# Leaving the future blocks out of the causal attention and the pooling of the mix stage

## The reference, cut to what matters

```python
def pool_mixer(u, w_pool, pool_scale):     # u: (B, S, 512), four groups, windows 2, 4, 8, 16
    for gi, w in enumerate(POOL_WINDOWS):
        # mean over the last w tokens (this one included) minus the token itself
        outs.append(((cs - prev) / cnt - ch).astype(u.dtype))
    mixed = jnp.einsum('bsgc,gcd->bsgd', pooled, w_pool)
    return mixed.reshape(B, S, POOL_WIDTH) * pool_scale

def dilated_branch(q, k, v, rel_bias, window, dil):
    """Causal attention over keys at distances 0, dil, 2*dil, ..., window."""
    ...
    band = (rel >= 0) & (rel <= w_sub)     # rel = query position minus key position
    s = jnp.where(mask, s, NEG_INF)
    ...

x = x + jnp.einsum('bse,ed->bsd', jnp.concatenate([a_out, b_out], axis=-1), w_out[i])
```

## Time and profile before

| | us |
|---|---|
| median of 3 runs | 2039.34 (2037.64 to 2043.03) |
| the profiled execution, its own time | 2040.03 |
| its span, first to last instruction | 2038.3 |
| TensorE busy | 1965.7 (96% of the span) |
| VectorE busy | 747.8 |
| ScalarE busy | 425.6 |
| mix stage, input product to the last output product | about 962 to 1070.5 |
| experts | about 1084.7 to 1995.8 |

### The profile page before, as it was taken

How to read it: one execution, slowest core, us unless ns; L and a number is a source line. 1 busy time by engine, 2 the same in 40 slices (tenths; PEclk the granted TensorE clock), 3 DMA queues, 4 the chain that set the end, 5 groups by cost and what they waited for, 6 DMA issues and landing times.

```text
span 2038.3 us, 26505 instructions
## 1 busy us (share of the span) xinstructions
PE 1965.7 (96%) x10834; PEld 1056.4 (52%) x10834; DVE 747.8 (37%) x2087; ACT 425.6 (21%) x1083; POOL 100.1 (5%) x84
## 2 busy tenths in 40 slices
PE   8999999999999999999999999999999999899997
PEld 7754567885865566885463333333333333333334
DVE  4569675212768677212143222211222122112213
ACT  2161465211042465211121000000000000000003
POOL 0021220000022121000000000000000000000000
PEclk9999999999999999999999999999999999999999
DMA  7633212343543312345859999999999999999992
GB/s 252 244 138 125 84 43 84 124 165 124 207 165 124 114 53 71 116 146 194 301 203 384 427 428 428 430 429 428 429 431 428 431 428 432 431 427 427 427 421 94
DMA packets 98820, 552.29 MB, mean 271 GB/s; under 512 B 8686, under 2 KB 13202, under 8 KB 77715
## 3 DMA queue, kind: packets, MB, share of 16 engines
q1 hardware_dynamic: 98706, 550.66, 67.1%
HBM read 547.43 MB, written 3.21 MB: 270 GB/s over the span
## 4 chain that ended last, share of the span: by engine, by line
PE 81%; DMA 16%; DVE 2%; ACT 1%; issue 1%; SPq 0%; DVEq 0%; ACTq 0%
PE bank L647 28%; DMA region<-w_gate_up_dram 15%; PE bank L1232 14%; PE bank L1264 8%; PE bank L770 6%; PE bank L1006 3%; PE bank L991 3%; PE bank L1175 2%; PE bank L1161 2%; PE bank L1090 1%; PE bank L1219 1%; DMA region<-w_in_dram 1%; PE bank L850 1%; PE bank L907 1%; PE bank L874 1%
## 5 line engine op out<-in xcount | busy, mean ns | idle before, releaser
L647 PE MATMUL bank<-region 128*128 128x256 f32 (+2 forms) x2352 | 607.6, 419 | 8.2 <-DMA region<-w_in_dram 4.4
L647 PEld LDWEIGHTS bank<-region 128*128 128x128 f32 x2352 | 442.1, 191 | 162.5 <-issue 110.3
L1232 PE MATMUL bank<-region 128*64 128x512 f32 x1872 | 415.0, 597 | 24.0 <-DMA region<-w_gate_up_dram 23.2
L1232 PEld LDWEIGHTS bank<-region 128*64 128x64 f32 x1872 | 130.8, 137 | 304.0 <-issue 262.3
L2339 DVE TENSOR_SCALAR region<-bank 128x512 f32<-128x512 f32 x32 | 22.1, 691 | 681.0 <-PE bank L1232 681.0
L1264 PE MATMUL bank<-region 128*64 128x512 f32 x944 | 209.9, 595 | 9.5 <-issue 8.0
L1264 PEld LDWEIGHTS bank<-region 128*64 128x64 f32 x944 | 77.1, 137 | 122.8 <-issue 122.8
L770 PE MATMUL bank<-region 128*128 128x512 f32 x256 | 129.2, 607 | 0.0
L1674 ACT ACTIVATE region<-region 128x512 f32<-128x512 f32 x32 | 20.2, 630 | 512.4 <-DVE region L2339 512.4
L1678 ACT ACTIVATE region<-bank 128x512 f32<-128x512 f32 x32 | 19.1, 597 | 326.8 <-PE bank L1264 326.8
L1835 DVE SCALAR_TENSOR_TENSOR region<-region,layer_mem 128x256 f32<-128x256 f32 x192 | 78.0, 477 | 0.0
(11 more groups left out here) (347 smaller groups left out, 1942.8 us busy)
## 6 DMA issues: line engine op xcount, KB each, us to landing
region<-w_gate_up_dram SPq DMA_DIRECT2D x32, 4096.0 KB, 39.0
region<-w_down_dram SPq DMA_DIRECT2D x59, 2048.0 KB, 34.3
region<-w_gate_up_dram SPq DMA_DIRECT2D x53, 2048.0 KB, 21.3
region<-w_in_dram SPq DMA_DIRECT2D x44, 2048.0 KB, 8.0
layer_mem<-w_gate_up_dram SPq DMA_DIRECT2D x11, 2048.0 KB, 35.1
region<-w_out_dram SPq DMA_DIRECT2D x6, 2048.0 KB, 8.4
layer_mem<-w_down_dram SPq DMA_DIRECT2D x5, 2048.0 KB, 36.1
region<-rows_scratch SPq DMA_DIRECT2D x4, 2048.0 KB, 9.3
```

What stands on the lines that cost most here:

```text
L647: mm = pe.matmul(dst, lhs(k), w(k), start=(k == 0), stop=(k == n_k - 1))
L1232: mm = pe.matmul(pb[g][hf * 64:(hf + 1) * 64, :], XT[:, 2 * (j % 2) + kk, j // 2, :], wj[:, kk, c:c + NB], start=(first and j == 0 and kk ...
```

## The change

`pair_pT` turns three of the four 128x128 blocks of each head: (kt, t) = (0, 0), (0, 1), (1, 1). They stand side by side in the first 384 columns of the bank, and `pair_aT` copies 128x384 where it copied 128x512. `pair_out` takes one key tile for the first query tile and two for the second. `pooling` takes the product of the second token tile over output tokens 128 to 255 only. Nothing else differs.

```diff
+CAUSAL = ((0, 0), (0, 1), (1, 1))
...
                 for m in range(2):
-                    for kt in range(NT):
-                        for t in range(NT):
-                            c = (kt * 2 + t) * P
-                            mm = pe.transpose(pb[(7, 0)[m]][:, c:c + P], p2[i % 2][:, m * 512 + t * S + kt * P:m * 512 + t * S + (kt + 1) * P], ident)
+                    for kt, t in CAUSAL:
+                        c = (kt + t) * P
+                        mm = pe.transpose(pb[(7, 0)[m]][:, c:c + P], p2[i % 2][:, m * 512 + t * S + kt * P:m * 512 + t * S + (kt + 1) * P], ident)
                 mm.then_inc(s("at_pT_ps"), 1)
...
                 for t in range(NT):
                     for m in range(2):
-                        mm = product(pb[1][:, t * P + m * 64:t * P + (m + 1) * 64], lambda kt: aT2[:, m * 4 + kt * 2 + t, :],
-                                     lambda kt: z2[:, 3, kt, i * P + m * 64:i * P + (m + 1) * 64], NT)
+                        mm = product(pb[1][:, t * P + m * 64:t * P + (m + 1) * 64], lambda kt: aT2[:, m * 3 + kt + t, :],
+                                     lambda kt: z2[:, 3, kt, i * P + m * 64:i * P + (m + 1) * 64], t + 1)
                 mm.then_inc(s("at_o_ps"), 1)
...
                 for g in range(4):
-                    mm = product(pb[2 + g // 2][:, (g % 2) * S:(g % 2 + 1) * S], lambda t: z2[:, 0, t, g * P:(g + 1) * P],
-                                 lambda t: band[:, t, g, :], NT)
+                    at = (g % 2) * S
+                    for t in range(NT):
+                        mm = pe.matmul(pb[2 + g // 2][:, at + t * P:at + S], z2[:, 0, t, g * P:(g + 1) * P], band[:, t, g, t * P:S],
+                                       start=(t == 0), stop=(t == 1), skip_group_check=True)
                 mm.then_inc(once("pool_ps"), 1)
...
                 for m in range(2):
-                    last = act.activation(aT2[:, 4 * m:4 * m + 4, :], units(pb[(7, 0)[m]][:, :]), ACT.Copy)
+                    last = act.activation(aT2[:, 3 * m:3 * m + 3, :], units(pb[(7, 0)[m]][:, 0:3 * P]), ACT.Copy)
                 last.then_inc(s("at_pT"), 1)
```

## The result

The changed kernel is slower, and the prediction was wrong in sign. Its median is 2043.49 us over 12 runs (2041.80 to 2048.05), that of the kernel before, run beside it, 2039.89 over 12 (2037.64 to 2043.03): a ratio of 1.0022, 95% interval 1.0014 to 1.003. The difference of the medians is 3.60 us. Forecast were 2035.9 and at most 2040.3.

A forecast was written before the change was run, and what follows sets the result against it. The prediction took the expert weight stream, started by TensorE's progress out of the mix stage, as the bound. Terms of 0.22 + 0.84 + 1.73 + 0 + 0.44 + 0.21 = 3.44 us took 2039.34 to 2035.9 us, range 2033.0 to 2040.3.

The forecast's parts named there:

- What bounds the kernel: Expert stage: the last expert ends when the weight stream ends, and that stream's start hangs on TensorE leaving the mix stage.
- pooling: Mix stage: four matmuls, eight instructions, halved to 128 columns; gain 0.84 us, bounds 0 and 0.9.
- each output product: Mix stage, `pair_out`: each of four pairs drops two matmuls, four instructions; gain 0.43 us each, 1.73 in all.
- transposes: Mix stage, `pair_pT`: each pair drops two; gain 0.22 us for the first pair, 0.44 for third and fourth together.
- the second pair's: Mix stage, second pair's transposes: gain 0, as the wait for ScalarE's last mixed row grows from 0.35 to 0.57 us.
- the copies: Mix stage, ScalarE's copies of turned weights: only the fourth pair's two count; gain 0.21 us, 0 to 0.25.
- isolated gap for a 64-column matmul: Output product: the skill's rule gives 29 ns each, for an estimated whole sum of about 2.2 us; set aside.
- Behind the mix stage the residual, the router and the first expert keep their lengths and start 3.4 us sooner: Behind the mix stage: the 3.4 us won passes on whole, also to the tile issued at 1088.40.
- No load or queue is moved past another: Mix stage: SyncE's waits come 1.5 to 3.4 us sooner, with nothing queued behind them in the DMA until 1069.71.
- The rival with the clock: Thinned mix stage: granted clock falls, 1.69 us a spell; from three spells slower, 2041.0 us; chance 0.07.
- The range: Whole kernel: 2033.0 to 2040.3 us, from a gain of 2.4 to 3.9 us, run scatter and the absorbed case.
- What would show it wrong: Clock under 1.00 from 1020 to 1085 us, pooling waiting for VectorE, full DMA queue at 1084, or last weight wait unmoved.

The follow-up runs named there:

- experiment 1: The changed kernel plus 48 TensorE instructions (12 tiny unread products) ahead of the router's product, in a wait for ScalarE: 2036.37 us, ratio 0.9988.
- experiment 9: The changed kernel plus 48 TensorE instructions (12 tiny products) behind the router's product: 2043.88 us, ratio 1.002.
- experiment 6: The changed kernel with the three expert tiles held until the router's product has ended, run once more with a profile: 2041.03 us.
- experiment 2: The kernel before, all blocks computed, plus 208 TensorE instructions (52 tiny products) ahead of a wait for ScalarE: 2039.97 us, ratio 1.0014.
- experiment 4: The changed kernel, TensorE's stream untouched, with SyncE issuing the three expert tiles only when x has been turned: 2043.42 us, ratio 1.0017.
- experiment 5: The changed kernel, TensorE's stream untouched, with SyncE holding the three expert tiles until the router's product has ended: 2041.28 us, ratio 1.0006.

## Why the prediction was wrong

- *What bounds the kernel* was right. The stream of expert weights follows TensorE out of the mix stage: the tile at 1088.40 went out at 1095.60 in the changed kernel, 7.2 us later, as the first expert began 7.2 us later (1091.90 against 1084.71). The stream's speed did not change, 429 GB/s:

```profile
1103.00:1473.00 370.00, 364.48 (x1762) 133.73 (x1758) 77.17 (x168) 25.21 (x42) 0.00 (x0) 1.00 1.01 429
```

- *The terms of the sum* were right: pooling 0.76 of 0.84, each output product 0.45 of 0.43, transposes 0.22, nothing from the second pair's (its wait went to 0.57), the copies 0.21; 3.41 of 3.44 us in the trace, and 3.3 us in the medians of experiment 1.
- *The Trainium skill's isolated gap for a 64-column matmul* ("TensorE: Matmul & The Clock Gate", "Back-to-back issue gap"), which I had set aside for the trace's 0.108 us, would have made the sum an estimated 2.2. The measured 3.41 sides with the trace.
- **The step that failed** is the sentence "Behind the mix stage the residual, the router and the first expert keep their lengths and start 3.4 us sooner". The router's product and the one behind it did not keep their lengths: a stall of 4.87 us in the first, 2.79 us of low clock in the second and 0.28 beside, 7.94 in the profiled run and 7.0 in a common one (experiment 9). I had also written "No load or queue is moved past another", having counted only the loads that the program issues. The program's own fetches are loads too, and removing 48 instructions moved one of them past three tiles of 2 MB.
- *The rival with the clock* forecast slower with a chance of 0.07, by a number near the measured one (2041.0), and for a wrong reason: from 1020 us to the turn of x the clock stayed at 1.00. A low clock is part of the loss, but it came with the stall: the clock fell in it or within 0.3 us behind it in all four traces that have one, and not there in the seven without.
- *The range* had an upper gain of 3.9 us that no term gives: the upper bounds stated for the pooling (0.9) and the copies (0.25) make 3.54. That did not matter. The range was too narrow, since it was built of sizes of terms and of scatter, and none of its cases had a stall that the trace of before does not show. "What would show it wrong" did name the place: a granted clock under 1.00 between 1020 and 1085 us.

## What to carry to other kernels

A change that takes instructions out moves every later block of the engine's program. Before it is costed, look where the next fetches fall: their queue in the page, its packets over the windows of the stage, and whether a stretch of very short instructions stands behind, since that is where an engine can run through a block faster than one is fetched (here 244 instructions in 1.24 us, against 2.4 us from the start of the packet until TensorE went on, in experiment 6). Then a few useless instructions in a wait ahead of it can be worth more than the change itself. Loads held back did not help here (experiments 4 to 6). And when a change makes a kernel slower by more than all that it touches, look for "issue" in the chain first.

## What the runs showed of the hardware that I had not expected

- The instruction queue had 86 packets of 16 KB for 22,023 recorded TensorE instructions before, and 87 for 22,231 in experiment 2: about one for 256.
- With empty DMA queues a block costs 2.1 us of stall where the router's product runs through one (experiment 6), behind three tiles 4.9 (changed kernel and experiment 9) to 5.7 us (experiment 4). So the cost of a block is not hidden here.
- The clock fell to 0.50 after the stall of 2.1 us too, and the product behind it took 5.32 us and not 3.63.
- When the block is asked for is not settled. The same program fetched it in the transposes of x in one run (experiment 5, no stall) and at the router's start in another (experiment 6). By the count of recorded instructions there are two moments and nothing between. In the seven traces without a stall the block's packet began when TensorE had started 12,953 to 12,977 instructions (less 256 in experiment 2, whose block is the next one), some 270 to 300 ahead of the edge. In the four with a stall it was 13,237 to 13,249, and the edge stands behind the 13,249th. The early case was the rule in experiment 2 (seven of twelve runs, by their times), and by their times one run in ten to twelve in experiments 4, 5 and 9, and none of twelve in the changed kernel. Why a run takes the one or the other stays open.
- The runs near 2048 us: in the profiled one of the changed kernel the 32 matmul instructions at the start of the second layer took 9.95 us, against 7.17 before, under a low clock, after a wait for weights that was as long in both (7.92 and 7.95 us):

```profile
487.81 7.92 DMA region<-w_in_dram
495.73 0.04 issue
495.77 9.95 PE bank L648 x32
```

It stands ahead of everything that the change touches and costs 2.8 us of the profiled execution. The profile of experiment 4 (2048.54 us) has the same, 10.13 us for these instructions, and that of experiment 9 (2042.38) has not, 7.17. The other two runs of the changed kernel near 2048 have no profile.
